# Two blocks of a transformer in one kernel: rows of peer_v gathered two heads behind those of peer_u, and nineteen of the last sums on VectorE

## What is computed

```python
def chunk(hc):
    q = (hc @ w_q).reshape(-1, PEER_HEADS, PEER_KEY_DIM)
    s1 = jnp.einsum('chd,nd->chn', q[..., :half], k1)
    s2 = jnp.einsum('chd,nd->chn', q[..., half:], k2)
    ...
    best_s, best_pos = lax.top_k(cand_s, PEER_TOPK)
    expert = jnp.take_along_axis(cand_i, best_pos, axis=-1)
    g = jax.nn.softmax(best_s, axis=-1)
    act = jax.nn.gelu(jnp.einsum('cd,chkd->chk', hc, u[expert]), approximate=False)
    wgt = g * act
    return jnp.einsum('chk,chkd->cd', wgt, v[expert])
```

## Time and profile before

| | us |
|---|---|
| median of three runs | 1568.42 (1565.18 to 1569.01) |
| the profiled execution, its own time | 1562.97 |
| its span, first to last instruction | 1561.1 |
| PE busy | 1354.9 (87%) |
| VectorE (DVE) busy | 850.4 (54%) |
| GpSimd (POOL) busy | 534.6 (34%) |
| ScalarE (ACT) busy | 301.0 (19%) |
| mean granted TensorE clock | 0.944 of full |

### The profile page before, as it was taken

The page is one execution under the profiler, slowest core; times in us unless marked ns, Lnnn a source line. Parts: engine busy times, 40 slices in busy tenths (PEclk is TensorE's granted clock), DMA queues, the critical chain, the costliest instruction groups (busy, mean ns, idle before and its releaser), DMA issues.

```text
span 1561.1 us, 14792 instructions
## 1 busy us (share of the span) xinstructions
PE 1354.9 (87%) x5270; PEld 887.1 (57%) x5270; DVE 850.4 (54%) x2010; ACT 301.0 (19%) x675; POOL 534.6 (34%) x545
## 2 busy tenths in 40 slices
PE   7999999999999999999858997889876777774976
PEld 6888888988587777665645543445322223221322
DVE  3458451243157777242586676666556566654445
ACT  2023101130100000144112233312301221121211
POOL 0001001200100000000063665656575666666664
PEclk9999999999999999998978998899988998987999
DMA  7343543304468887473398999899999999999997
GB/s 285 110 164 134 199 151 108 109 1 147 144 244 299 301 302 250 132 266 126 109 368 319 410 360 367 324 401 405 348 401 356 355 362 390 388 357 361 377 365 290
DMA packets 172041, 424.78 MB, mean 272 GB/s; under 512 B 14723, under 2 KB 57145, under 8 KB 171713
## 3 DMA queue, kind: packets, MB, share of 16 engines
q0 software_dynamic: 73760, 268.49, 44.5%
q1 hardware_dynamic: 98208, 155.35, 28.3%
HBM read 422.74 MB, written 1.06 MB: 271 GB/s over the span
## 4 chain that ended last, share of the span: by engine, by line
PE 65%; issue 9%; POOL 6%; DMA 6%; DVE 5%; another core or an unknown queue 5%; ACT 3%; SPq 0%; DVEq 0%; ACTq 0%; POOLq 0%
PE psum L582 29%; PE psum L1051 13%; POOL wr L2435 4%; PE psum L833 4%; DMA wr<-in_peer_v,arena 2%; PE psum L903 2%; POOL arena L2435 2%; PE psum L809 2%; PE psum L887 1%; DMA arena<-in_w_out 1%; PE psum L1020 1%; PE psum L879 1%; DVE wr L2247 1%; PE psum L630 1%
## 5 line engine op out<-in xcount | busy, mean ns | idle before, releaser
L582 PE MATMUL psum<-hT,wr 128*128 128x256 f32 x1792 | 393.5, 382 | 1.6 <-DVE hT L1611 1.6
L1051 PE MATMUL psum<-wr,arena 128*128 128x512 f32 x656 | 322.8, 634 | 81.1 <-ACT arena L1476 32.3
L582 PEld LDWEIGHTS psum<-hT,wr 128*128 128x128 f32 x1792 | 342.3, 191 | 51.9 <-issue 5.3
L2247 DVE CUSTOM_DVE_ANT_0 wr<-psum,wr 128x1024 f32<-128x1024 f32 x184 | 224.4, 1219 | 141.6 <-DMA wr<-in_peer_u,arena 127.2
L1051 PEld LDWEIGHTS psum<-wr,arena 128*128 128x128 f32 x656 | 125.9, 202 | 259.4 <-issue 203.8
L2435 POOL DMA_INDIRECT wr<-in_peer_u,arena x184 | 172.7, 939 | 230.1 <-DVE arena L2191 125.4
L2435 POOL DMA_INDIRECT wr<-in_peer_v,arena x169 | 159.5, 944 | 86.8 <-issue 44.6
L1051 PE MATMUL psum<-arena 128*128 128x512 f32 x260 | 137.1, 672 | 55.4 <-issue 37.5
L1476 ACT ACTIVATE arena<-cst,arena 128x128 f32<-128x128 f32 x245 | 84.3, 393 | 267.7 <-PE psum L1051 118.6
L1051 PEld LDWEIGHTS psum<-arena 128*128 128x128 f32 x260 | 52.2, 213 | 139.5 <-issue 124.1
L2406 POOL TENSOR_TENSOR arena<-arena 128x512 f32<-128x512 f32 x11 | 16.9, 1538 | 229.7 <-DVE arena L1626 229.7
(11 more groups left out here) (330 smaller groups left out, 1456.8 us busy)
## 6 DMA issues: line engine op xcount, KB each, us to landing
wr<-in_w_in SPq DMA_DIRECT2D x22, 2048.0 KB, 8.4
arena<-in_w_ada SPq DMA_DIRECT2D x12, 2048.0 KB, 9.7
wr<-in_w_up SPq DMA_DIRECT2D x22, 1024.0 KB, 7.9
wr<-in_w_down SPq DMA_DIRECT2D x5, 2048.0 KB, 8.9
arena<-in_w_in SPq DMA_DIRECT2D x8, 1024.0 KB
wr<-in_w_a_out SPq DMA_DIRECT2D x2, 2048.0 KB, 8.1
wr<-in_w_b_out SPq DMA_DIRECT2D x2, 2048.0 KB, 8.4
wr<-in_w_o SPq DMA_DIRECT2D x2, 2048.0 KB, 7.7
```

The lines of the kernel that those rows point to most:

```text
L582: mm = nc.tensor.matmul(bank[p % 4][:, f * S:(f + 1) * S], slot(i)[:, k, c:c + P], act[:, k, :], start=k == 0, stop=k == KT - 1)
L1051: mm = nc.tensor.matmul(bank[(6, 0)[t] + half][:, :], diag[:, PE_AT[n] % DIAGS, :], gring[slot_of][:, half * BANK:(half + 1) * BANK], star ...
L2247: V.tensor_tensor_reduce(gring[slot_of], h2[t], gring[slot_of], 1.0, 0.0, ALU.mult, ALU.add, dots[:, t, c:c + 1]).then_inc(s["dot_done"], 1)
```

## The change

Two numbers are changed. `lag` begins at two heads instead of one, so it is 32 to 40; and `ON_DVE` begins at 216, so it has nineteen sets.

```diff
-ON_DVE = tuple(range(232, 254, 2))
+ON_DVE = tuple(range(216, 254, 2))
...
 def lag(n):
-    return PK + min(max((n - 40) // 8, 0), 8)
+    return 2 * PK + min(max((n - 40) // 8, 0), 8)
```

## The result

| | before | after |
|---|---|---|
| median of six runs, us | 1567.38 (1564.62 to 1569.01) | 1579.31 (1571.15 to 1583.04) |
| ratio, 95% interval | | 1.007 (1.0045 to 1.0095) |
| profiled execution, own time (span) | 1562.97 (1561.1) | 1583.04 (1581.2) |
| PE, VectorE, POOL busy in it | 1354.9, 850.4, 534.6 | 1348.6, 857.8, 538.3 |

The account below looks back on a forecast made before the run. From about 780 us on, POOL's pace in issuing 512 gathers was taken as the bound. Terms 0 - 13 - 13 + 1 + 20.3 = -4.7, say -5, from the 1568.42 median gave 1563, range 1550 to 1580.

Parts of the forecast that it names:

- The start, ticks 0 to 20: nothing.: VectorE's first dot products (one per tick): tick 20 unmoved, within 3 us either way, POOL having issued 29 gathers in both.
- Ticks 20 to 33: 13 less.: Rows of u already in the slots, so VectorE goes at its own pace: 29 us instead of 42.
- Ticks 33 to 64: 13 less.: With 22 to 26 sums on PE instead of 30, the stretch takes 76 us instead of 88.9.
- After, PE has no arrears: Ticks 33 to 64: PE, 1 to 5 sums done at tick 33, needs only 68 to 75 us.
- are paid for below: Gathers not issued by tick 33 (place 46 instead of 55 gathers issued) are charged later in the forecast.
- Rival 2: Ticks 33 to 64 keep their 88.9, set by attention's chain on four engines: +8, 1577; chance 0.18.
- Ticks 64 to 255: 1 more.: Same gathers; new wait of 10.7 for v127 at tick 164's add, not stopping POOL, costed at 1.
- The end: 20.3 more.: After u255, 41 gathers of v remain instead of 25: sixteen more at 1.27 each.
- the cost of the eight sums on POOL's issues: At the end, VectorE's eight added sums delay POOL's issues by 0; up to 10 if they used a two-port mode.
- Rival 1 (bytes): The gathers' bytes are the bound wherever they stand, so the change gives 0: 1568; chance 0.22.

Follow-up runs that it names:

- second pair: Second profiled pair: the unchanged kernel before, run again (ratio 1.001), and the changed kernel, run again (1.0049 to the kernel before).
- pair at level 1499: Kernel before and changed kernel, both with PE's sums of v one tick sooner, profiled where the kernel before took 1499; medians 1514.57 and 1522.98.
- c2_change_sums_sooner: Changed kernel with PE's sums of v one tick sooner in its program; ratio 1.0153 to the kernel before.
- labels a, c and f: Follow-up runs whose names begin with a, c or f, on chips 2, 10 and 11; the kernel before took 1499 in them.
- a4_close_later: Changed kernel with tile 0's close 16 ticks later (add at tick 180, last norm at 196); ratio 1.0037 to the kernel before.
- c1_before_sums_sooner: Kernel before with PE's sums of v one tick sooner in its program; ratio 1.0113 to the kernel before.

## Why the prediction was wrong

*The start, ticks 0 to 20: nothing.* Right (48.2 both times; 48.2 and 51.0 in the second pair, just inside the 3 allowed).

*Ticks 20 to 33: 13 less.* Right in size and by its reason: 14.1 and 16.2 less in the two pairs (6.2 in the pair at level 1499).

*Ticks 33 to 64: 13 less.* **This is the step that failed**, and it alone turns the sum from -5 to +8. It measured +2.7 and -0.2, and at level 1499 5.5 less. "After, PE has no arrears" was the fault in it. Two things were left out. Up to the first logits PE is held by the pieces of weights: it waits 15.7 for three of them, runs the projections behind them partly at the lower clock (29.6 instead of 21.9), and its last projection stands behind tick 33. So the sixteen sums, removed from it, bring the logits 11.6 earlier and no more; VectorE, 15.5 ahead at tick 33, waits for them. From tick 33 to the logits it is 14.4 now, and was 10.6. This half is read from the traces; no run has the weights earlier. And behind the logits there was no debt to pay off: PE's order has the same sums between the same steps, 105 records to tick 64 in both, in 78.3 and 77.2 us. The pair at level 1499 says the same: 77.0 and 76.9 from the logits to tick 64, so that all of its 5.5 lies between tick 33 and the logits. I subtracted sums by counting from a time (30 sums in 89 us of before, "22 to 26" after) where the order ties them to a place: four of the 30 stood ahead of the logits, and the other 26 are there in both. The later runs agree with PE and ACT's order as what leads: sums sooner cost about 1% with or without the change, a slot less nothing in sum.

The missing gathers "are paid for below", I wrote, and priced them at the end's 1.27. That price was right; it is the saving that was too small for it. Sixteen gathers out of the start saved 10 to 12 us in POOL's issue of u40 (0.6 to 0.8 each, since POOL stood still there for longer instead: 41 against 25), and cost 1.245 at least wherever they went. Rival 2, "after tick 33 the ticks keep their pace", named the step and what speaks for it, the sums tied to the attention's steps, and gave 1577; 1579 was measured. That the two are so near is partly luck: rival 2 puts the change at +8, the medians at +12, and its other two steps came out too small as well.

*Ticks 64 to 255: 1 more.* It was 8.8 and 6.6. The add at tick 164 waits 29.5 in the first profile (the trace puts the row of v127's sum 16 earlier than VectorE's start) and POOL stands 7.8 to 8.6 beyond its pace behind it, in all four profiles with that wait at level 1568; the standstill at this time costs POOL 4.2 and 6.0 in the two profiles of before as well. So 2 to 4 of it are the wait's. At level 1499 the wait is 12.0, or 11.5 in `c2_change_sums_sooner`, and costs POOL nothing, as forecast (10.7); in the pair there the whole stretch is 514.5 and 514.6, so the step is right where the standstills are missing. At level 1568 the rest stays open; two profiles of the kernel before differ by 4.4 in this stretch.

*The end: 20.3 more.* 23.9 and 22.6, and 20.0 at level 1499. The gathers' part was right; the cost of the eight sums on POOL's issues, set to 0, is 2.4 to 3.3 by the two pairs at level 1568.

Rival 1 (bytes) does not explain it: a start that moves 310 GB/s where it moved 373 (833 to 875) is not short of bandwidth, and the result is no zero. One reading in the prediction is off without a consequence: from 780 on, go from 290 to 410 GB/s, not from 324 to 405.

## What to carry to other kernels

When one queue must issue a fixed number of transfers, measure a stage by the place its queue has reached at a given time, not by how early the consumer is. Here the consumer was 12 us early at tick 64, yet at 951 us the queue had issued 99 gathers where it had issued 105 before, and at 1100 us 185 for 198. Taking work out of a stage saves only up to the next thing that is late there (here pieces of weights on their way to PE, and the clock that its waiting cost), and work that is moved from a stage where it is partly hidden to one that runs at the queue's pace costs the full price. On an engine with a fixed order, count work between places of that order, never between times.

## What was not expected of the hardware

*One kernel, two levels.* The kernel before took 1499 for the labels a, c and f and 1568 to 1572 for the others. All of POOL's issues beyond 1100 in `a4_close_later`, at level 1499 (stretch; then POOL's longest sums of waiting, total, times, longest):

```profile
1100.00:1420.00 320.00, 251.01 (x501) 97.88 (x502) 208.93 (x522) 70.66 (x164) 241.89 (x257) 0.91 1.03 416
...
POOL wr L2435 <- issue: 41.5, 136, 0.3
POOL arena L2435 <- issue: 34.5, 113, 0.3
```

No single wait is over 0.3, and the DMA engines move 416 GB/s over 320 us. At level 1568 the same stretch has 361 to 371, and POOL, VectorE and ACT stand still together at about the same ticks in both kernels, some twelve times from 950 on (1126, 1179, 1211, 1245, 1279 before; 1124, 1177, 1212, 1243, 1278 after), 1.5 to 6 us for POOL each time. PE's semaphore for sums then shows three to eight updates within half a microsecond, mostly after 4 to 31 us without one, although PE's rows go on. One of these bursts, seven updates at 1278.1, comes just ahead of the add at tick 164 (1278.24); the wait there is 28.1 to 29.5 in four profiles at this level and 11 to 12 in two at the other. What causes the standstills no run here shows. The traces themselves differ too: at level 1568 they hold only about half of the semaphore updates (6565 in that of before, 13065 in `c1_before_sums_sooner`), and 205 of the 245 of PE's sums, so whoever is named there as having ended a wait is less sure, and a part of the recording in the standstills can't be ruled out. Nor are they all of the difference: ticks 0 to 20, ahead of the first of them, take 36 instead of 47 to 51. The Trainium skill (Perfetto Trace Analysis, "Roofline") gives 358 GB/s of HBM bandwidth as a core's share and about 120% of that as the practical ceiling with one core active; by that 416 is 116%, and the trace agrees. The 358 that rival 1 took for a limit is none here.

*POOL's issue and VectorE's sum.* Two sums of line 2349 beside the long issues shown above:

```profile
1531.55 1.28 DVE L2349 SCALAR_TENSOR_TENSOR arena<-wr,arena 128x1024 f32<-128x1024 f32 x1 [2.18 <-DMA wr<-in_peer_v,arena]
...
1546.82 1.28 DVE L2349 SCALAR_TENSOR_TENSOR arena<-arena 128x1024 f32<-128x1024 f32 x1 [1.17 <-issue]
```

The issue that began at 1531.73 ended at 1533.65, 0.82 behind the end of the sum (1532.83); the one of 1547.14 at 1548.91, 0.81 behind 1548.10. Fifteen issues of this profile began while such a sum was running. Eleven of them ended 0.81 behind that sum; the other four began in its last 0.13 and took 0.94, as did those that began before a sum. The product (line 2346) is another case: an issue that had begun 0.38 before it was held too, until 0.12 behind its end, and 0.12 it is in eleven profiles. The Trainium skill (SBUF — State Buffer, "SBUF: two separate sides") says that GpSimd and VectorE share a pair of ports as an exclusive lock, held for a whole instruction so that the other "fully blocks", and that an instruction of VectorE with two SBUF inputs takes it against a GpSimd operation that reads SBUF. For the sums, which have two inputs in SBUF, the trace agrees. That whichever starts first has the pair does not fit the product. With nineteen such sums it cost 3.6 in this profile and 5.2 in its repeat, with eleven 0.3 and 2.8; at level 1499 0.1 to 0.9, since there nearly every issue had begun ahead of its sum or in its last 0.13.
